# A transformer layer on one core: half-width fp32r matmuls joined to 512 columns in merge, output and down projections

## The reference

```python
def merge_branches(p, y_rwkv, ...):
    y_gmlp = chunk_mlp(p[..., RWKV_COLS:OFF_GATES], ln_v_g, ln_v_b, w_spatial, b_spatial)
    gate_a, gate_b = jnp.split(p[..., OFF_GATES:], 2, axis=-1)
    m = jax.nn.sigmoid(gate_a) * (y_rwkv @ w_proj_a) + jax.nn.sigmoid(gate_b) * (y_gmlp @ w_proj_b)
    return m @ w_out
...
    x = x + gt1 * rmsnorm(mix, g_post1)
    h2 = rmsnorm(x, g_pre2) * (1.0 + sc2) + sh2
    x = x + gt2 * rmsnorm(conv_glu_ffn(h2, w_up, conv_ffn, w_down, grid=True), g_post2)
```

## Time and profile before

| | us |
|---|---|
| median of 3 timed runs (3061.09 to 3066.61) | 3062.55 |
| profiled execution, its own time | 3067.53 |
| its span in the trace | 3065.8 |
| TensorE busy over the span | 2886.9 (94%) |
| VectorE busy | 1912.8 (62%) |
| ScalarE busy | 936.5 (31%) |
| merge, TensorE's first matmul to its last | 1813.4 to 2138.2 |
| out, first to last matmul of a product | 2143.6 to 2244.2 |
| up | 2268.0 to 2783.6 |
| down | 2783.6 to 3046.7 |
| 2800 to 3000 us: TensorE, VectorE, ScalarE busy | 200.0, 80.3, 75.5 |
| same stretch: granted clock, DMA share | 1.00, 0.53 |
| TensorE's last sum of squares in a norm (two records, 3047.42) | 0.70 |
| ScalarE's Exp of 128x256 in a norm (2249.81) | 0.42 |

### The profile page before, as it was taken

The page is one execution under the profiler, slowest core; times in us unless marked ns, Lnnn a source line. Parts: engine busy times, 40 slices in busy tenths (PEclk is TensorE's granted clock), DMA queues, the critical chain, the costliest instruction groups (busy, mean ns, idle before and its releaser), DMA issues.

```text
span 3065.8 us, 70044 instructions
## 1 busy us (share of the span) xinstructions
PE 2886.9 (94%) x27808; PEld 2215.2 (72%) x27808; DVE 1912.8 (62%) x3548; ACT 936.5 (31%) x1619; POOL 439.0 (14%) x580
## 2 busy tenths in 40 slices
PE   5899999999999999999999899999989999999997
PEld 1245555566555566555666499999979999999997
DVE  1116667777667777677776364444368898896444
ACT  1112212222222222222221243333354444443333
POOL 0001111111111111101111030000013333331000
PEclk8799999999999999999999999999989999999998
DMA  7621322123322223322214545555435555554553
GB/s 307 265 80 61 104 96 85 63 77 97 104 90 77 70 80 101 104 90 68 68 60 138 188 152 176 186 178 185 159 130 178 184 186 178 181 187 156 179 176 133
DMA packets 75290, 412.27 MB, mean 134 GB/s; under 512 B 9200, under 2 KB 11888, under 8 KB 42736
## 3 DMA queue, kind: packets, MB, share of 16 engines
q1 hardware_dynamic: 74352, 407.51, 38.6%
q0 software_dynamic: 768, 2.10, 0.2%
HBM read 405.38 MB, written 4.19 MB: 134 GB/s over the span
## 4 chain that ended last, share of the span: by engine, by line
PE 85%; DVE 7%; issue 4%; DMA 3%; ACT 2%; SPq 0%; DVEq 0%; ACTq 0%; PEldq 0%
PE PB L668 20%; PE Q L920 6%; PE Q L921 6%; PE Q L925 6%; PE PB L920 4%; PE PB L921 4%; PE PB L925 4%; PE CH L925 3%; PE CH L921 3%; PE CH L920 3%; DMA ring<-w_mod_dram 2%; PE PB L653 2%; PE Q L791 2%; PE Q L805 2%; PE CH L832 2%
## 5 line engine op out<-in xcount | busy, mean ns | idle before, releaser
L668 PE MATMUL PB<-hT,ring 128*128 128x512 f32 (+1 forms) x1536 | 705.2, 569 | 6.4 <-PEq L657 5.4
L1627 DVE TENSOR_TENSOR w_lo_r<-ring,w_hi_r 128x1536 fp32r<-128x1536 f32 (+3 forms) x178 | 387.5, 2177 | 270.5 <-ACT w_hi_r L1212 270.5
L1212 ACT ACTIVATE w_hi_r<-ring 128x2048 fp32r<-128x2048 f32 (+2 forms) x178 | 325.8, 1831 | 453.9 <-PE Q L925 211.7
L668 PEld LDWEIGHTS PB<-hT,ring 128*128 128x128 f32 x1536 | 256.0, 192 | 97.3 <-issue 45.6
L921 PE MATMUL PB<-hT_r,w_hi_r 128*128 128x256 f32 x832 | 204.5, 285 | 0.0
L1787 DVE TENSOR_TENSOR w_lo_r<-ring,w_hi_r 128x1408 fp32r<-128x1408 f32 x62 | 101.2, 1633 | 148.0 <-ACT w_hi_r L1326 148.0
L1485 DVE SCALAR_TENSOR_TENSOR arena<-ring,csilp,arena 128x512 f32<-128x512 f32 x240 | 180.1, 750 | 4.0
L920 PE MATMUL PB<-hT_r,w_hi_r 128*128 128x256 f32 x704 | 175.7, 289 | 4.7 <-DVE hT_r L1714 4.7
L920 PE MATMUL Q<-ff_hi_r,w_hi_r 128*128 128x256 f32 x704 | 175.7, 288 | 1.8 <-ACT w_hi_r L1326 1.8
L921 PE MATMUL Q<-ff_lo_r,w_hi_r 128*128 128x256 f32 x704 | 172.9, 284 | 0.0
L920 PE MATMUL CH<-hT_r,w_hi_r 128*128 128x256 f32 x704 | 170.9, 283 | 0.0
(11 more groups left out here) (264 smaller groups left out, 5996.6 us busy)
## 6 DMA issues: line engine op xcount, KB each, us to landing
ring<-w_up_dram SPq DMA_DIRECT2D x88, 1024.0 KB, 4.8
ring<-w_mod_dram SPq DMA_DIRECT2D x128, 512.0 KB, 3.7
ring<-w_rkv_dram SPq DMA_DIRECT2D x48, 1024.0 KB, 6.0
ring<-w_down_dram SPq DMA_DIRECT2D x64, 704.0 KB, 4.0
ring<-w_mod_dram SPq DMA_DIRECT2D x32, 1024.0 KB, 8.1
ring<-w_ga_dram SPq DMA_DIRECT2D x16, 1024.0 KB, 4.8
ring<-w_gb_dram SPq DMA_DIRECT2D x16, 1024.0 KB, 4.8
ring<-w_pa_dram SPq DMA_DIRECT2D x16, 1024.0 KB, 4.8
```

The costliest lines, as they stand in the source:

```text
L668: last = mm(PB[slot % 2][:, 0:cols], tile(n, kt), hT[:, kt, 0:cols], start=(kt == 0), stop=(kt == KT - 1))
L1212: f(w_hi_r[:, r % 2, 0:n], ring[:, r, 0:n], ACT.Copy).then_inc(hi_rdy, 1)
L1627: tt(w_lo_r[:, r, 0:n], ring[:, r, 0:n], as_f32(w_hi_r[:, r % 2, 0:n]), ALU.subtract).then_inc(lo_rdy, 1)
```

## The change

The high and the low part of an activation now lie side by side or in one tensor (`m_r`, `yr_r`, `yg_r`, `ff_r`, each with a dimension of two; for h the high part is copied by ScalarE in four pieces into `hT_r[:, :, 0:T]`, next to the low part). In merge, out and down one matmul of 512 columns (`high_pair`) takes the place of L920 and L921 and fills a whole bank; the low weights' matmul adds into the half that belongs to the activation's high part. Stages gu and up keep two matmuls of 256. VectorE then adds the two halves of the bank with one `tensor_reduce` from PSUM (`halves`), into the gates, the products of merge, or mixT. ScalarE takes the sigmoid and the squares from SBUF, and its copy out of PSUM is gone. The table that holds both Ln and Exp is loaded explicitly ahead of the norm of v, ahead of out and ahead of down.

```diff
+            def high_pair(bank, r, k, both, start):
+
+                mm(bank[:, :], w_hi_r[:, r % 2, k * P:(k + 1) * P], both, start=start, stop=False)
...
+            pe.wait_ge(hr_rdy, 4)
+            pe.sem_inc(me_sum, 2)
...
                     if r < 2:
-                        pe.wait_ge(me_act, i * 2 + r + 1)
+                        pe.wait_ge(me_sum, i * 2 + r + 1)
...
                     for kt in range(n):
-                        with_high(Q[r][:, 0:T], r, kt, hi[:, kt], lo[:, kt], kt == 0)
+                        high_pair(Q[r], r, kt, both[kt], kt == 0)
                     low_ready("merge", i, r)
                     for kt in range(n):
-                        last = with_low(Q[r][:, 0:T], r, kt, hi[:, kt], kt == n - 1)
+                        last = with_low(Q[r][:, half * T:(half + 1) * T], r, kt, hi[:, kt], kt == n - 1)
...
-                    pe.wait_ge(o_sb, i * 4 + r + 1)
+                    pe.wait_ge(o_sum, i * 4 + r + 1)
...
+            act.preload_act_table_set("natural_log_exp_and_others")
             act.wait_ge(gv_st, 2)
...
+                    if i == 1:
+                        act.wait_ge(hl_rdy, 1)
+                        f(h_in_r[:, 4 * r:4 * r + 4], as_f32(h_hi_r[:, 4 * r:4 * r + 4]), ACT.Copy).then_inc(hr_rdy, 1)
...
                     if r < 2:
-                        product(r, "merge", 0, i, 1)
-                        f((sga, sgb)[r], Q[r][:, 0:T], ACT.Sigmoid).then_inc(me_act, 1)
+                        act.wait_ge(me_sum, i * 2 + r + 3)
+                        f((sga, sgb)[r], (sga, sgb)[r], ACT.Sigmoid).then_inc(me_act, 1)
...
-                    product(r, "out", 0, i, 1)
+                    act.wait_ge(o_sum, i * 4 + r + 5)
                     to = bass.ds(i * 4 + r, 1)
-                    f(mixT[:, to, :].rearrange("p a b -> p (a b)"), four[r][:, 0:T], ACT.Copy)
-                    f(sq[:, to, :].rearrange("p a b -> p (a b)"), four[r][:, 0:T], ACT.Square).then_inc(o_sb, 1)
-
+                    f(sq[:, to, :].rearrange("p a b -> p (a b)"), mixT[:, to, :].rearrange("p a b -> p (a b)"),
+                      ACT.Square).then_inc(o_sb, 1)
+
+            act.preload_act_table_set("natural_log_exp_and_others")
             fours(4, out_four)
...
+            def halves(out, bank):
+
+
+                return nc.vector.tensor_reduce(out, bank[:, :].rearrange("p (a b) -> p b a", a=2), mybir.AxisListType.X, ALU.add)
...
             with dve.Fori(0, 3) as i:
                 for r in range(4):
                     low("out", i, r + 2)
+                    out_sum(i, r)
```

More of the change, by code:

```diff
@@ L963, in _ @@
                     if r < 2:
-                        pe.wait_ge(me_act, i * 2 + r + 1)
+                        pe.wait_ge(me_sum, i * 2 + r + 1)
                     else:
                         pe.wait_ge(m_rdy, i + 1)
-                    hi, lo, n = ((h_hi_r, h_lo_r, KT), (h_hi_r, h_lo_r, KT), (yr_hi_r, yr_lo_r, KT), (yg_hi_r, yg_lo_r, GG))[r]
+                    n = GG if r == 3 else KT
+                    if r < 2:
+                        both, hi, half = [hT_r[:, kt] for kt in range(n)], h_hi_r, 0
+                    else:
+                        pair, hi, half = ((yr_r, yr_hi_r, 1), (yg_r, yg_hi_r, 0))[r - 2]
+                        both = [pair[:, :, kt] for kt in range(n)]
                     for kt in range(n):
-                        with_high(Q[r][:, 0:T], r, kt, hi[:, kt], lo[:, kt], kt == 0)
+                        high_pair(Q[r], r, kt, both[kt], kt == 0)
                     low_ready("merge", i, r)
                     for kt in range(n):
-                        last = with_low(Q[r][:, 0:T], r, kt, hi[:, kt], kt == n - 1)
+                        last = with_low(Q[r][:, half * T:(half + 1) * T], r, kt, hi[:, kt], kt == n - 1)
                     last.then_inc(used[r], 1)
             pe.wait_ge(m_rdy, KT + 1)
+            pe.sem_inc(o_sum, 4)
             pe.sem_inc(o_sb, 4)
@@ L1028, in _ @@
                 up_four(i, False)
+            pe.sem_inc(dn_sum, 2)
             pe.sem_inc(dn_sb, 2)
@@ L1671, in merge_four @@
                     lows("merge", i, r, KT, "out")
-                    if r >= 2:
+                    product(r, "merge", 0, i, 1)
+                    if r < 2:
+                        halves((sga, sgb)[r], Q[r]).then_inc(me_sum, 1)
+                    else:
                         o, g = ((mta, sga), (mtb, sgb))[r - 2]
-                        product(r, "merge", 0, i, 1)
-                        dve.wait_ge(me_act, i * 2 + r + 1)
-                        m = V.tick(tt(o, g, Q[r][:, 0:T], ALU.mult))
+                        flow(halves(o, Q[r]))
+                        dve.wait_ge(me_act, i * 2 + r - 1)
+                        m = V.tick(tt(o, o, g, ALU.mult))
                 V.need(m)
@@ L1685, in _, with out_sum @@
             merge_four(KT - 1)
+            def out_sum(i, r):
+                product(r, "out", 0, i, 1)
+                halves(mixT[:, bass.ds(i * 4 + r, 1), :].rearrange("p a b -> p (a b)"), four[r]).then_inc(o_sum, 1)
             with dve.Fori(0, 3) as i:
@@ L1787, in low_down, with down_sum @@
                 tt(w_lo_r[:, r, 0:n], ring[:, r, 0:n], as_f32(w_hi_r[:, r % 2, 0:n]), ALU.subtract).then_inc(lo_rdy, 1)
+            def down_sum(i, q):
+                product(3, "down", q, i, 2)
+                halves(mixT[:, bass.ds(i * 2 + q, 1), :].rearrange("p a b -> p (a b)"), Q[2 + q]).then_inc(dn_sum, 1)
             with dve.Fori(0, KT // 2 - 1) as i:
```

42 lines of the change are left out of this document (26 added, 16 removed).

## The result

The changed kernel takes **3044.71 us** (median of 5 runs, 3041.57 to 3050.91), the kernel before 3062.55 (5 runs beside it, 3061.09 to 3068.36). The ratio is 0.9941 with a 95% interval of 0.9923 to 0.9959. Faster, as forecast, but by 18 us and not by 44, and outside the range of 3011 to 3040.

A forecast was written before the change was run, and what follows sets the result against it. TensorE's own matmul stream was taken to bound merge, output and down. -44.4 from joined matmuls and +1.4 +0.4 -1.75 +1.8 -1.4 at the joints sum to -43.95, giving 3018.6 us, range 3011 to 3040.

The forecast's parts named there:

- The step of a joined matmul: Merge, output, down: 512 fp32r columns take 215.8 ns, 24.2 less than two of 256; 1834 pairs bring -44.4 us.
- five numbers: Matmul costs read for the step: fp32r 256 columns at both clocks; fp32 256, 512 and 128 columns at 2.4 GHz.
- the first rival: Merge, output, down: 13.3 ns paid once per matmul whatever its length, step 226.6 ns, total 3038.4 us; chance 0.12.
- the row that I held against the rival: fp32r matmul of 256 columns at 1.2 GHz: its excess vanishes, as a floor's would.
- the longer standstill: Start of down: the moved table load delays the high split; TensorE idle about 3.5 us, +1.8 us in all.
- The count of pairs: Merge, output, down: one pair per weight tile, 1856 together, some 22 of them at 1.2 GHz without gain.
- No stall in merge or output: Merge hides reductions up to about 0.9 us; output's square fits with 0.17 us to spare; cost 0.
- The joints: Between stages: merge to output +1.4, first norm +0.4, second norm -1.75, up to down +1.8, last norm -1.4 us.
- the first case: The forecast itself holds, with its own bounds reaching from 3011 to 3025 us; chance 0.68.
- The dearer reduction: VectorE's reduction takes 1.16 us; merge stalls 0.95 us an iteration, 19 us given back, 3038 us; chance 0.08.
- the step of 240: Merge, output, down: 512 columns step at 240.0 ns, only the joints are left, 3063 us; chance 0.07.
- the exposed weight load: Ahead of long matmuls the weight load is uncovered: step 320 ns, +147 us, 3209 us; chance 0.04.

The follow-up runs named there:

- e1: Changed kernel leaving out part of the columns in output, down and merge's projections, to test other matmul widths; one execution 2979.4 us.
- e2: Changed kernel with the high and low parts of down's weights and activation in bf16, less exact; one execution 3029.63 us.
- e5: Kernel before with only the change's three early table loads (v norm, output, down); 3065.01 us against 3066.17, ratio 0.9994.
- e9: Changed kernel run again, unchanged, for a second trace; 3049.13 us, ratio 0.9939 to the kernel before.
- e3: Changed kernel with VectorE's reductions reading each half of the bank twice, so sums are doubled; one execution 3057.0 us.

## Why the prediction was off, step by step

**The step of a joined matmul is what failed**: "a small fixed cost and a floor that a long stream covers fit all five numbers; the floor I take for the weight load". It measured 226.7 ns, not 215.8 (after, e1, e2). That is the first rival's 226.6, and I had given it a chance of 0.12. The five numbers fitted two formulas. I let three fp32 rows decide over one fp32r row, although the format was the very thing in which they differed; e2 shows that it decides. And the row that I held against the rival was no evidence against it. At 1.2 GHz 256 columns stream for 213.3 ns and show no excess; if a stream of that length covered a floor, 512 columns at 2.4 GHz, which stream just as long, would show none either. They show 13.3. So in fp32r the excess is there at 2.4 GHz and gone at 1.2, also where the stream is equally long (213 ns), and its absence at 1.2 GHz was no sign of a floor. 1834 x 10.9 ns = **20 us** of the 25 that are missing in the stages from the u product on (-44 forecast, -19.3 measured).

The other 5:
- **The head of a series**, not in the forecast: about 20 ns a series net, 144 series, 2.9 us. It is there in fp32r at 512 columns and gone in bf16.
- **The clock at the start of down**, 1.1 us (2.6 of slow clock in place of 1.5): I priced the longer standstill rightly (3.47 us) and did not ask what the granted clock does behind it.
- **The u product**, 0.5 us: the one VectorE step of 0.95 us. Every trace with the joined layout has it (50.33 us), before and e5 have not (49.80). It lies ahead of the copies of h, which cost nothing, as I had said. Why the step takes twice as long is open: GpSimd's split of yg runs beside it in both kernels and now writes to the joined tensor, but no run tests that alone.

By stage, with 0.0133 us a pair and 0.02 a series: merge some 885 x 0.0133 less 64 x 0.02 = -10.5 (measured -10.55); down -9.4 + 1.7 of standstill + 1.1 of clock + 1.3 of series = -5.3 (-5.15); output -3.3 + 0.3 = -3.0 (-2.67, -2.87 in e9).

**What held.** That TensorE's stream alone bounds merge, output and, behind the first tile, down. The count of pairs (L935 ran 704 times in down). The reduction, 0.68 us for the 0.69 taken from a multiplication of 512 elements. No stall in merge or output, and the high split for product 2 ready about 2 us early (2.3 us in the changed kernel's trace, 1904.97 against 1907.25); that reductions can outgrow merge (e3), though the wait then comes at another tile. That 512 columns bring nothing at 1.2 GHz. The joints: +1.36 for +1.4, -1.22 for -1.35, -1.36 for -1.4, and a standstill of 3.47 us for 3.5.

**The rivals.** "Paid once per matmul" was the case, and it still was too low: its own sum from the profiled execution, 3067.5 - 24.1 = 3043.4, lies 6.8 us under the 3050.2 measured, 4.5 by the three terms above and 2.0 in the unchanged part ahead, which is within what that part varies by. Three figures beside the forecast do not add up and decided nothing: 0.95 us in each of 16 iterations is 15 us, not 13 to 14; 0.53 - 0.429 is 101 ns, not 104; and joints off by 3 us end the first case at 3022, not 3025. The dearer reduction, the step of 240 and the exposed weight load didn't occur. The range ended at that rival's own time with nothing beyond it, so its small terms put the result outside.

## What to carry to other kernels

Price a matmul of a new width from rows of the same number format; rows of another format can fit a formula and still not share its constant. If two formulas fit all the rows, look for two rows that share what one formula calls the cause (here a stream of 213 ns at either clock) and differ in the effect, before giving one of them most of the chance. When a step is queued ahead of another engine's next input, move what the waiting engine needs to the front of the queue, and then find what ends last in its place: here that was worth 3.3 us at one joint at once, and at the next one only after a second change (0.6, then 3.0).

## What the runs showed of the hardware that I had not expected

- At the full clock an fp32r matmul costs 13.3 ns over its columns at 256, 320, 384 and 512 columns, 16.7 at 448; in bf16, at 256 and 512 columns, 2.5 ns. At 1.2 GHz neither 256 nor 512 columns of fp32r pay anything (213 and 426 ns).
- Below 256 columns fp32r has a floor: 192 and 128 columns both step at about 111 ns.
- A weight load is recorded at 191 ns in fp32r and at 98 ns in bf16 (means from 2850 to 2950 us). Groups by line of the changed kernel:

```profile
L930 PEld LDWEIGHTS Q<-ff_r,w_lo_r 128*128 128x128 f32 x275 | 36.3, 191 | 1.9
```

And of e2:

```profile
L1069 PEld LDWEIGHTS Q<-ff_b,w_lo_b 128*128 128x128 bf16 x300 | 29.3, 98 | 9.4
```

- Whether the granted clock is 0.50 behind a standstill of TensorE is not set by its length alone: of two kernels that stood still 3.46 us at the same place one lost 2.6 us and the other nothing, and of four that stood still 2.04 us one lost nothing and three 1.5 to 1.6.
